# One PSUM bank for the last three scale/shift sums, and the steps around it, in a fused fp32 transformer kernel

## The chip, the core and the metric

The kernel runs on one core of a Trainium2 chip. The metric is the device time of one execution in microseconds (us), taken as the median of several. The profile adds one execution in which the hardware profiler recorded every instruction. TensorE is called PE in it, VectorE DVE, ScalarE ACT, GpSimd POOL, and SyncE, which issues the weight loads, SP.

## What is computed

A first block (adaptive-norm transformer block with two attention branches and an MLP) is followed by a second one of two layers (SwiGLU feed-forwards, a pooling mixer, latent attention). The sequence has 256 tokens, the width is 1024, and from the second block on 16 meta tokens stand ahead of the 256. The change touches the second half of the first block and its handover:

```python
mod = cs @ ada_w[l] + ada_b[l]
shift1, scale1, gate1, shift2, scale2, gate2 = jnp.split(mod, N_MOD, axis=-1)
...
merged = jax.nn.sigmoid(ga) * ya + jax.nn.sigmoid(gb) * yb
x = x + gate1[:, None, :] * (merged @ w_out[l])
h2 = modulate(rmsnorm(x, norm2_g[l]), shift2, scale2)
y = jnp.square(jax.nn.relu(h2 @ w_mlp_in[l])) @ w_mlp_out[l]
x = x + gate2[:, None, :] * y
...
h = jnp.concatenate([meta, x], axis=1)
h = h + 0.5 * swiglu(rmsnorm_2(h, ffn1_norm[l]), ffn1_w_gate[l], ffn1_w_up[l], ffn1_w_down[l])
```

Everything is fp32.

## The kernel before

**Precision and weights.** Each fp32 factor is split into a high part (fp32r) and the remainder, and a product is made of three matmuls (lines 564 to 566): high by high, remainder by high, high by remainder. The weights are one stream of chunks of 128x1024 values (512 KB), in the order of use. SP loads chunk c into slot c mod 8 of `raw`. ACT writes the high part of a chunk into `whi` (line 1010), DVE the remainder into `wlo` (line 1343); both have 5 slots. The chunks that are split carry their own numbers ("split 44" is chunk 84). The chunks of `ada_w` are not split: DVE multiplies them by the conditioning vector and sums (`ada_piece`, lines 1363 and 1366), two products a chunk. SP loads chunk c only when chunk c-8 has been consumed: for a split chunk by its `wlo`, for one of `ada_w` by its two products. SP's loads are one queue in order, so one that waits holds back all behind it.

**Groups.** A matrix product is cut into groups of two output tiles, each 128 outputs by 256 tokens: `wout0` to `wout3` (8 input tiles, 48 matmuls, two chunks each), `mlp_in0` to `mlp_in15` (48 matmuls, two chunks), `mlp_out0` to `mlp_out3` (32 input tiles, 192 matmuls, eight chunks). A group's sums lie in one of two PSUM pairs, G0 and G1. `pair_plan` lists all users of the pairs in order, they take them in turn, and `pair(name)` makes PE wait until the user two places earlier has been read by DVE (or ACT). Behind a group, DVE reads it: for `wout` and `mlp_out` this is `residual` (line 1397), then ACT makes `xh` (line 1031) and DVE `xl` (line 1404), the two parts of the next input; for `mlp_in` it is a scaling with `rstd` (line 1581).

**Scale/shift sums.** `mod7`, `mod10` and `mod11` are the last three of eight groups of columns of `mod` summed in this way (mod7 belongs to shift2, mod10 and mod11 to gate2). `mod_sum` on PE turns the 128x512 partial sums by four transposes (line 600) into PSUM; `mod_out` on DVE reduces them (line 1377) and adds the bias (line 1379). They are users of the pairs: mod7 stands behind wout1, mod10 behind mlp_in7, mod11 behind mlp_out0. So the group that follows each of them gets the pair of the group that ended just before it: wout2 that of wout1, mlp_in8 that of mlp_in7, mlp_out1 that of mlp_out0. Four more banks, A0 to A3, serve the attention, the means and the first gate/up group (`gu01`) of each SwiGLU, which uses A1 and A2.

**What sets the order.** Each engine's program is written out by hand; the engines meet by semaphores. `splits(name)` issues the splits up to a number that the plan gives for that group (`hi_to`, `lo_to`), so that ACT and DVE run ahead of PE. In wout0 DVE first makes the gain (`mod_gain`), then the ada piece (7, 3) (chunk 81), then the remainders of splits 44, 45 and 46 (the two chunks of wout1 and the first of wout2). ACT loads the table of Sqrt (`preload`) ahead of the high parts of splits 45 to 47. The meta tokens are scaled, split and squared on DVE and ACT in mlp_out0's turn, between `mod_out("mod11")` and the residual of mlp_out0, since all residuals of mlp_out wait for mod11. The groups after these are mlp_in0 behind wout3 (its first chunk is split 50) and mlp_in1 (its first chunk is split 52).

Of the kernel before, what the change touches and what calls it, by code (L numbers as in the profile page):

```python
# [251 lines left out]
MOD_ORDER = ["mod4", "mod5", "mod8", "mod9", "mod6", "mod7", "mod10", "mod11"]  # L252
HEAD_MODS = {4: "mod5", 8: "mod8", 12: "mod9", 16: "mod6"}
# [19 lines left out]
def pair_plan():  # L273
# [10 lines left out]
    out += [("wout0", 0, 2), ("wout1", 0, 2), ("mod7", 0, 1), ("wout2", 0, 2), ("wout3", 0, 2)]  # L284
    for i in range(FF1 // 2):
        out += [(f"mlp_in{i}", 0, 1)] + ([("mod10", 0, 1)] if i == 7 else [])
    out += [("mlp_out0", 0, 2), ("mod11", 0, 1)] + [(f"mlp_out{i}", 0, 2) for i in (1, 2, 3)]
# [21 lines left out]
class Plan:  # L309


    def __init__(self):
# [37 lines left out]
        order = [u[0] for u in users]  # L350
        for first, then in (("mod7", "wout1"), ("mod10", "mlp_in7"), ("mod11", "mlp_out0")):
            order.remove(first)
            order.insert(order.index(then), first)
        by = {u[0]: u for u in users}
        a = d = 0
        for name in order:
            a, d = a + by[name][1], d + by[name][2]
            self.left_act[name], self.left_dve[name] = a, d


def build_program(nc, xT, metaT, vecs, consts, bias_oh, bias_rows, wstream, scratch, outT):
# [6 lines left out]
    with ctx:  # L368
# [89 lines left out]
        out_done, mod_set = sem("out_done"), sem("mod_set")  # L458
# [81 lines left out]
        def tensor_program(e):  # L540
# [53 lines left out]
            def mod_sum(name, i, n=1):  # L594
                out = pair(name)
                for t in range(4 * n):
                    if t % 4 == 0:
                        e.wait_ge(ada_total, ADA_ORDER.index(i + t // 4) + 1)
                    acc = ada_sets[ADA_SET[i + t // 4]][0][:, t % 4 * P:(t % 4 + 1) * P]
                    m = e.transpose(out[:, 0, t * P:(t + 1) * P], acc, ident)  # L600
                m.then_inc(mod_summed, 1)
# [149 lines left out]
            for i in range(4):  # L751
                g = pair(f"mlp_out{i}")

                def ready(kt):
                    if i == 0 and kt % 2 == 0:
                        e.wait_ge(hid_lo, kt // 2 + 1)
                gemm(f"mlp_out{i}", [g[:, t, 0:SEQ] for t in range(2)], hid1, ready)
                if i == 0:
                    mod_sum("mod11", 11)
# [36 lines left out]
            e.wait_ge(pT1_done, HEADS1)  # L796
# [202 lines left out]
        def scalar_program(e):  # L999
# [123 lines left out]
            for i in range(4):  # L1123
                splits(f"brb{i}")
                if i:
                    merged_high(i - 1)
            merged_high(3)


            preload(ACT.Sqrt)  # L1130
            for i in range(4):
                splits(f"wout{i}")
                if i == 0:
                    e.wait_ge(gain_done, 2)
                if i == 1:
# [30 lines left out]
            for i in range(4):  # L1166
                splits(f"mlp_out{i}")
                if i == 0:
                    e.wait_ge(meta_scaled, 1)
                    e.activation(xh[:, :, 0:META], scaled_m, ACT.Copy).then_inc(meta_hi, 1)  # L1170
                    e.wait_ge(gain_done, 3)
# [162 lines left out]
        def vector_program(e):  # L1334
# [39 lines left out]
            def mod_out(name, n=1):  # L1374
                i = int(name[3:])
                e.wait_ge(mod_summed, MOD_ORDER.index(name) + 1)
                e.tensor_reduce(mod[:, 4 * i:4 * i + 4], G[plan.pair[name]][:, 0, :].rearrange("p (t d) -> p t d", t=4), AX_X, ALU.add).then_inc(left_dve, 1)
                e.wait_ge(left_dve, plan.left_dve[name])
# [151 lines left out]
            for i in range(4):  # L1530
# [19 lines left out]
            for i in range(4):  # L1550
                if i == 0:
                    ada_piece(*ADA_BRANCH[3])
                splits(f"wout{i}")
# [12 lines left out]
            for i in range(FF1 // 2):  # L1566
# [5 lines left out]
                if i == 7:  # L1572
                    mod_out("mod10")
# [8 lines left out]
                if i:  # L1582
                    hidden_low(i - 1)
            hidden_low(FF1 // 2 - 1)
# [4 lines left out]
            for i in range(4):  # L1589
                splits(f"mlp_out{i}")  # L1590
                if i == 0:
                    mod_out("mod11")
# [9 lines left out]
                    e.wait_ge(left_dve, plan.left_dve["mod11"])  # L1602
                residual("mlp_out", i, COLS1, lambda kt: mod[:, 5 * KT + kt:5 * KT + kt + 1])
                x_lo("ffn1_0", i, COLS1, lambda kt: g1m[:, kt:kt + 1])

# [447 lines left out]
```

## Time and profile before

| | us |
|---|---|
| median of 3 executions | 1317.89 |
| lowest, highest | 1317.29, 1320.47 |
| the profiled execution | 1315.07 |
| its span from first to last record | 1313.7 |

| engine | busy us | share of the span |
|---|---|---|
| PE | 1245.2 | 95% |
| DVE | 898.9 | 68% |
| ACT | 632.7 | 48% |
| POOL | 183.5 | 14% |

A row of the timeline gives start and duration in us, the engine, the line, the operation with its output and inputs, how many instructions it stands for, and in brackets how long the engine sat idle before it and what released it. Matmuls overlap in the array, so a matmul's duration is longer than its distance to the next; the distance from start to start is the time it costs. PEclk is the granted clock of PE, 1.00 being 2.4 GHz and 0.50 being 1.2 GHz.

### The profile page before, as it was taken

Reading aid. Unit: us, or ns where it says so; the run is one execution under the profiler, and the core shown is the slowest. Engines: PE = TensorE matmul, PEld = TensorE weight load, DVE = VectorE, ACT = ScalarE, POOL = GpSimd, SP = SyncE. Lnnn points to the kernel's source line nnn. Section 1 sums busy time; section 2 is a strip of 40 time slices with the busy share of each in tenths; the row PEclk is TensorE's granted clock in tenths of the full one; section 3 lists DMA queues with packets and bytes.
Section 4 is the critical chain, followed back from the end, with each engine's and each line's share of the span. In section 5 each row is a group of like instructions: output and inputs, shape, how many; then the busy total and the mean of one; then the engine's idle time right before and its main releaser. Section 6 shows DMA issues by size and latency. Waiting matters only on the chain.

```text
span 1313.7 us, 23695 instructions
## 1 busy us (share of the span) xinstructions
PE 1245.2 (95%) x9876; PEld 1210.4 (92%) x9876; DVE 898.9 (68%) x1283; ACT 632.7 (48%) x973; POOL 183.5 (14%) x181
## 2 busy tenths in 40 slices
PE   4999998999999999999799999989999999999996
PEld 3988898999899999999799999989999977999996
DVE  7969888777456766655966666676666664866653
ACT  4545544666344444443544444444445454644531
POOL 2014524000123000012300001210001220000022
PEclk7999999999999999999899999989999998999998
DMA  8956564666665555555245565445655531556540
GB/s 324 379 198 213 198 236 145 243 222 241 184 187 161 161 189 167 178 175 177 79 160 179 175 191 172 154 142 193 193 186 184 187 119 49 178 192 193 181 157 32
DMA packets 66994, 238.87 MB, mean 182 GB/s; under 512 B 7302, under 2 KB 9528, under 8 KB 66888
## 3 DMA queue, kind: packets, MB, share of 16 engines
q1 hardware_dynamic: 66296, 235.17, 53.7%
q0 software_dynamic: 592, 2.19, 0.5%
q8 instruction: 78, 1.28, 0.4%
q14 instruction: 28, 0.23, 0.0%
HBM read 236.26 MB, written 1.07 MB: 181 GB/s over the span
## 4 chain that ended last, share of the span: by engine, by line
PE 83%; DVE 11%; ACT 2%; issue 2%; DMA 1%; POOL 1%; SPq 0%; DVEq 0%; ACTq 0%
PE G L564 25%; PE G L565 25%; PE G L566 25%; DVE sb_wlo L1343 3%; DVE sb_hidf L1426 1%; DMA sb_raw<-in_wstream 1%; PE G L584 1%; DVE sb_rstd L1389 1%; PE A L691 1%; PE A L667 1%; ACT sb_whi L1010 1%; DMA sb_X<-in_xT 0%; DVE sb_xl L1846 0%; PE A L584 0%; ACT sb_p L1306 0%
## 5 line engine op out<-in xcount | busy, mean ns | idle before, releaser
L1343 DVE TENSOR_TENSOR sb_wlo<-sb_raw,sb_whi 128x1024 fp32r<-128x1024 f32 x395 | 488.5, 1269 | 94.0 <-ACT sb_whi L1010 93.7
L564 PE MATMUL G<-sb_xh,sb_whi 128*128 128x256 f32 (+2 forms) x1764 | 503.0, 285 | 13.7 <-DVE sb_gu L1634 7.5
L565 PE MATMUL G<-sb_xl,sb_whi 128*128 128x256 f32 (+2 forms) x1764 | 502.0, 285 | 0.0
L566 PE MATMUL G<-sb_xh,sb_wlo 128*128 128x256 f32 (+2 forms) x1764 | 500.6, 284 | 0.0
L1010 ACT ACTIVATE sb_whi<-sb_raw 128x1024 fp32r<-128x1024 f32 x395 | 404.6, 1050 | 197.9 <-PE G L566 169.2
L564 PEld LDWEIGHTS G<-sb_xh,sb_whi 128*128 128x128 f32 x1764 | 333.7, 189 | 17.6 <-DVE sb_gu L1634 8.4
L566 PEld LDWEIGHTS G<-sb_xh,sb_wlo 128*128 128x128 f32 x1764 | 333.6, 189 | 0.0
L565 PEld LDWEIGHTS G<-sb_xl,sb_whi 128*128 128x128 f32 x1764 | 333.3, 189 | 0.1
L564 PE MATMUL G<-sb_hh,sb_whi 128*128 128x256 f32 (+1 forms) x1056 | 300.2, 284 | 8.9 <-DVE sb_X L1397 6.3
L566 PE MATMUL G<-sb_hh,sb_wlo 128*128 128x256 f32 (+1 forms) x1056 | 299.4, 283 | 0.0
L565 PE MATMUL G<-sb_hl,sb_whi 128*128 128x256 f32 (+1 forms) x992 | 280.9, 283 | 0.0
L564 PEld LDWEIGHTS G<-sb_hh,sb_whi 128*128 128x128 f32 x1056 | 200.0, 189 | 9.9 <-DVE sb_X L1397 6.8
L566 PEld LDWEIGHTS G<-sb_hh,sb_wlo 128*128 128x128 f32 x1056 | 199.9, 189 | 0.0
L565 PEld LDWEIGHTS G<-sb_hl,sb_whi 128*128 128x128 f32 x992 | 187.3, 189 | 0.0
L1194 ACT ACTIVATE sb_gu<-sb_gu 128x272 f32<-128x272 f32 (+1 forms) x88 | 37.4, 425 | 196.5 <-DVE sb_gu L1634 194.0
L1634 DVE TENSOR_TENSOR sb_gu<-G,sb_rstd 128x544 f32<-128x544 f32 (+1 forms) x84 | 59.4, 707 | 63.3 <-PE G L566 63.3
L1874 POOL TENSOR_TENSOR sb_sumsq<-sb_X 128x256 f32<-128x256 f32 (+1 forms) x6 | 3.7, 620 | 700.4 <-DVE sb_X L1397 700.4
L1638 DVE TENSOR_TENSOR sb_hidf<-sb_gu 128x272 f32<-128x272 f32 (+1 forms) x88 | 38.2, 434 | 49.9 <-ACT sb_gu L1194 49.9
L1641 DVE TENSOR_TENSOR sb_hl<-sb_hidf,sb_hh 128x272 fp32r<-128x272 f32 (+1 forms) x88 | 38.2, 434 | 43.2 <-ACT sb_hh L1196 43.2
L1879 POOL TENSOR_TENSOR sb_sq<-sb_X 128x256 f32<-128x256 f32 (+1 forms) x42 | 33.0, 786 | 206.9 <-DVE sb_X L1397 206.9
L1196 ACT ACTIVATE sb_hh<-sb_hidf 128x272 fp32r<-128x272 f32 (+1 forms) x88 | 37.4, 424 | 49.6 <-DVE sb_hidf L1638 49.6
L1882 POOL TENSOR_TENSOR sb_sumsq<-sb_sumsq,sb_sq 128x256 f32<-128x256 f32 (+1 forms) x43 | 47.4, 1102 | 3.4
(299 smaller groups left out, 1276.8 us busy)
## 6 DMA issues: line engine op xcount, KB each, us to landing
sb_raw<-in_wstream SPq DMA_DIRECT2D x443, 512.0 KB, 4.4
sb_bias<-bias_scratch POOLq DMA_DIRECT2D x1, 2048.0 KB, 16.7
sb_X<-in_xT SPq DMA_DIRECT2D x2, 512.0 KB, 6.5
out_T<-sb_X SPq DMA_DIRECT2D x4, 256.0 KB, 2.2
sb_con<-in_consts SPq DMA_DIRECT2D x1, 632.0 KB, 7.3
sb_vec<-in_vecs SPq DMA_DIRECT2D x1, 82.5 KB, 1.9
sb_X<-in_metaT POOLq DMA_DIRECT2D x1, 64.0 KB, 4.7
sb_boh<-in_bias_oh SPq DMA_DIRECT2D x1, 51.0 KB
```

Source lines behind the costliest of these rows:

```text
L564: e.matmul(out, w_h, xs, start=k0 + s.kt == 0, stop=False)
L565: e.matmul(out, w_h, xr, start=False, stop=False)
L566: m = e.matmul(out, w_l, xs, start=False, stop=k0 + s.kt == ktotal - 1)
L1010: e.activation(whi[:, i % NSPLIT, 0:w], raw[:, c % NRAW, 0:w], ACT.Copy).then_inc(hi_done, 1)
L1194: e.activation(gu[:, b, 0, 0:n], gu[:, b, 0, 0:n], ACT.Silu).then_inc(silu_done, 1)
L1196: e.activation(hh[:, j * n:(j + 1) * n], hidf[:, b, 0:n], ACT.Copy).then_inc(hid_hi, 1)
L1343: e.tensor_tensor(wlo[:, i % NSPLIT, 0:w], raw[:, c % NRAW, 0:w], f(whi[:, i % NSPLIT, 0:w]), ALU.subtract).then_inc(lo_done, 1)
L1634: e.tensor_tensor(gu[:, b, :, 0:n], G[plan.pair[name]][:, :, 0:n], rb, ALU.mult).then_inc(left_dve, 1)
L1638: e.tensor_tensor(hidf[:, b, 0:n], gu[:, b, 0, 0:n], gu[:, b, 1, 0:n], ALU.mult).then_inc(hid_mul, 1)
L1641: e.tensor_tensor(hl[:, sl], hidf[:, b, 0:n], f(hh[:, sl]), ALU.subtract).then_inc(hid_lo, 1)
L1879: e.tensor_tensor(s, src, src, ALU.mult).then_inc(sumsq_done, 1)
L1882: e.tensor_tensor(sumsq[:, cols], sumsq[:, cols], s, ALU.add).then_inc(sumsq_done, 1)
```

## The change

It has four parts.

1. `mod7`, `mod10` and `mod11` leave the list of the pairs' users and get bank A2. PE waits for `pT1_done` (the attention's last read of that bank) ahead of mod7 and for `mod_read` (DVE's reduction of the one before) ahead of the others; the first SwiGLU waits for three of `mod_read`. Three users fewer means that each group from wout2 on waits for the group two places earlier, and that the groups between the three change pairs.
2. On DVE, mod10's reduction moves behind the scaling of mlp_in7 and the remainder of mlp_in6. On PE, mod11's transposes move from behind mlp_out0 to behind mlp_out1, and on DVE its reduction to behind `x_lo` of mlp_out1. The residuals of mlp_out0 and mlp_out1 wait for mod10's result alone, those of mlp_out2 and mlp_out3 for mod11's.
3. In wout0, DVE makes the three remainders ahead of the ada piece; ACT makes its three high parts ahead of the load of the Sqrt table, which goes to wout3. `split_hi` and `split_lo` up to wout0's last chunk are also called ahead of `merged_high(3)` and `merged_low(3)`.
4. The meta tokens' four steps on DVE and one on ACT move from mlp_out0's turn to mlp_out1's.

```diff
+OWN_BANK = ("mod7", "mod10", "mod11")
...
-    out += [("wout0", 0, 2), ("wout1", 0, 2), ("mod7", 0, 1), ("wout2", 0, 2), ("wout3", 0, 2)]
+    out += [("wout0", 0, 2), ("wout1", 0, 2), ("wout2", 0, 2), ("wout3", 0, 2)]
     for i in range(FF1 // 2):
-        out += [(f"mlp_in{i}", 0, 1)] + ([("mod10", 0, 1)] if i == 7 else [])
-    out += [("mlp_out0", 0, 2), ("mod11", 0, 1)] + [(f"mlp_out{i}", 0, 2) for i in (1, 2, 3)]
+        out.append((f"mlp_in{i}", 0, 1))
+    out += [(f"mlp_out{i}", 0, 2) for i in range(4)]
...
             def mod_sum(name, i, n=1):
-                out = pair(name)
+                if name in OWN_BANK:
+                    out = A[2][:, :].unsqueeze(1)
+                    if name == OWN_BANK[0]:
+                        e.wait_ge(pT1_done, HEADS1)
+                    else:
+                        e.wait_ge(mod_read, OWN_BANK.index(name))
+                else:
+                    out = pair(name)
...
-                if i == 0:
+                if i == 1:
                     mod_sum("mod11", 11)
...
-            e.wait_ge(pT1_done, HEADS1)
+            e.wait_ge(mod_read, len(OWN_BANK))
             swiglu("ffn1_0", final_factor)
...
+            split_hi(steps["wout0"][-1].i)
             merged_high(3)
...
-            preload(ACT.Sqrt)
             for i in range(4):
                 splits(f"wout{i}")
                 if i == 0:
                     e.wait_ge(gain_done, 2)
+                if i == 3:
+                    preload(ACT.Sqrt)
...
                 splits(f"mlp_out{i}")
                 if i == 0:
+                    e.wait_ge(gain_done, 3)
+                if i == 1:
                     e.wait_ge(meta_scaled, 1)
                     e.activation(xh[:, :, 0:META], scaled_m, ACT.Copy).then_inc(meta_hi, 1)
-                    e.wait_ge(gain_done, 3)
...
+            split_lo(steps["wout0"][-1].i)
             merged_low(3)
...
             for i in range(4):
+                splits(f"wout{i}")
                 if i == 0:
                     ada_piece(*ADA_BRANCH[3])
-                splits(f"wout{i}")
...
-                if i == 7:
-                    mod_out("mod10")
...
                 if i:
                     hidden_low(i - 1)
+                if i == 7:
+                    mod_out("mod10")
...
-                if i == 0:
-                    mod_out("mod11")
+                if i == 1:
                     mx, mg = X[:, :, 0:META], V("ffn1_norm0", 0, KT).unsqueeze(2).broadcast_to([P, KT, META])
...
-                    e.wait_ge(left_dve, plan.left_dve["mod11"])
+                if i == 0:
+                    e.wait_ge(mod_set, MOD_ORDER.index("mod10") + 1)
+                if i == 2:
+                    e.wait_ge(mod_set, MOD_ORDER.index("mod11") + 1)
                 residual("mlp_out", i, COLS1, lambda kt: mod[:, 5 * KT + kt:5 * KT + kt + 1])
                 x_lo("ffn1_0", i, COLS1, lambda kt: g1m[:, kt:kt + 1])
+                if i == 1:
+                    mod_out("mod11")
```

What moves on DVE at wout0, before. `sb_sc` and `sb_p` with `sb_raw` are the two products of the ada piece, `sb_wlo` the remainders of the weights; the row of `sb_X` is the residual of wout0.

```order
285 L1384 TENSOR_TENSOR sb_g1m<-sb_g1m,sb_vec 128x8 [waits gain_done]
286 L1366 SCALAR_TENSOR_TENSOR sb_sc<-sb_raw,sb_csil,sb_sc 128x512 [waits ada_acc,loaded1]
287 L1366 SCALAR_TENSOR_TENSOR sb_p<-sb_raw,sb_csil,sb_p 128x512 [waits ada_acc]
288 L1372 TENSOR_TENSOR sb_sc<-sb_sc,sb_p 128x512 [waits ada_acc]
289 L1343 TENSOR_TENSOR sb_wlo<-sb_raw,sb_whi 128x1024 [waits hi_done] x3
290 L1397 SCALAR_TENSOR_TENSOR sb_X<-G,sb_mod,sb_X 128x256 [waits mm_done]
```

The same stretch of DVE now:

```order
285 L1394 TENSOR_TENSOR sb_g1m<-sb_g1m,sb_vec 128x8 [waits gain_done]
286 L1349 TENSOR_TENSOR sb_wlo<-sb_raw,sb_whi 128x1024 [waits hi_done] x3
287 L1372 SCALAR_TENSOR_TENSOR sb_sc<-sb_raw,sb_csil,sb_sc 128x512 [waits ada_acc,loaded1]
288 L1372 SCALAR_TENSOR_TENSOR sb_p<-sb_raw,sb_csil,sb_p 128x512 [waits ada_acc]
289 L1378 TENSOR_TENSOR sb_sc<-sb_sc,sb_p 128x512 [waits ada_acc]
290 L1407 SCALAR_TENSOR_TENSOR sb_X<-G,sb_mod,sb_X 128x256 [waits mm_done]
```

The three remainders stand ahead of the ada piece; nothing is added, and no split stands ahead of `mod_gain` that was not there before.

What moves on DVE between mlp_out0 and mlp_out1, before (`sb_mod<-G` is mod11's reduction, the rows down to `sb_sumsq` the meta tokens):

```order
393 L1343 TENSOR_TENSOR sb_wlo<-sb_raw,sb_whi 128x1024 [waits hi_done] x8
394 L1377 TENSOR_REDUCE sb_mod<-G 128x4 [waits mod_summed]
395 L1379 TENSOR_TENSOR sb_mod<-sb_mod,sb_vec 128x4 [waits left_dve]
396 L1596 TENSOR_TENSOR sb_hidf<-sb_X,sb_vec 128x128 [waits hid_lo,meta_in]
397 L1598 TENSOR_TENSOR sb_xl<-sb_hidf,sb_xh 128x8x16 [waits meta_hi]
398 L1599 TENSOR_TENSOR sb_hidf<-sb_X 128x128
399 L1601 TENSOR_REDUCE sb_sumsq<-sb_hidf 128x16 [waits meta_sq]
400 L1397 SCALAR_TENSOR_TENSOR sb_X<-G,sb_mod,sb_X 128x256 [waits mm_done,left_dve]
```

The same stretch now, on to the end of mlp_out1's turn:

```order
393 L1349 TENSOR_TENSOR sb_wlo<-sb_raw,sb_whi 128x1024 [waits hi_done] x8
394 L1407 SCALAR_TENSOR_TENSOR sb_X<-G,sb_mod,sb_X 128x256 [waits mm_done,mod_set]
395 L1407 SCALAR_TENSOR_TENSOR sb_X<-G,sb_mod,sb_X 128x256
396 L1414 SCALAR_TENSOR_TENSOR sb_xl<-sb_X,sb_g1m,sb_xh 128x256 [waits xh_done] x2
397 L1349 TENSOR_TENSOR sb_wlo<-sb_raw,sb_whi 128x1024 [waits hi_done] x8
398 L1606 TENSOR_TENSOR sb_hidf<-sb_X,sb_vec 128x128 [waits hid_lo,meta_in]
399 L1608 TENSOR_TENSOR sb_xl<-sb_hidf,sb_xh 128x8x16 [waits meta_hi]
400 L1609 TENSOR_TENSOR sb_hidf<-sb_X 128x128
401 L1611 TENSOR_REDUCE sb_sumsq<-sb_hidf 128x16 [waits meta_sq]
402 L1407 SCALAR_TENSOR_TENSOR sb_X<-G,sb_mod,sb_X 128x256 [waits mm_done]
403 L1407 SCALAR_TENSOR_TENSOR sb_X<-G,sb_mod,sb_X 128x256
404 L1414 SCALAR_TENSOR_TENSOR sb_xl<-sb_X,sb_g1m,sb_xh 128x256 [waits xh_done] x2
```

The residual of mlp_out0 is now the first thing behind the eight remainders; the meta tokens and mod11 stand behind the next eight.

## Rows read from the trace of the kernel before

**Rows 1.** The page: busy us of each engine, share of span, instructions

```profile
PE 1245.2 (95%) x9876; PEld 1210.4 (92%) x9876; DVE 898.9 (68%) x1283; ACT 632.7 (48%) x973; POOL 183.5 (14%) x181
```

**Rows 2.** PE's timeline, last matmul of wout0, first of wout1

```profile
201.41 0.28 PE L566 MATMUL G<-sb_hh,sb_wlo 128*128 128x256 f32 x1
...
203.58 0.35 PE L564 MATMUL G<-sb_hh,sb_whi 128*128 128x256 f32 x1 [1.89 <-DVE sb_wlo L1343]
```

**Rows 3.** PE's timeline, mod7's transposes and the start of wout2

```profile
209.27 0.60 PE L600 MATMUL G<-sb_con,sb_sc 128*128 128x128 f32 x4
212.90 0.39 PE L564 MATMUL G<-sb_hh,sb_whi 128*128 128x256 f32 x1 [3.03 <-DVE sb_X L1397]
...
216.64 0.31 PE L564 MATMUL G<-sb_hh,sb_whi 128*128 128x256 f32 x1
```

**Rows 4.** PE's timeline, mod10's transposes and the start of mlp_in8

```profile
272.10 0.60 PE L600 MATMUL G<-sb_con,sb_gu 128*128 128x128 f32 x4
274.35 0.38 PE L564 MATMUL G<-sb_xh,sb_whi 128*128 128x258 f32 x1 [1.66 <-DVE sb_hidf L1581]
```

**Rows 5.** PE's timeline, mod11's transposes and the start of mlp_out1

```profile
342.73 0.60 PE L600 MATMUL G<-sb_con,sb_gu 128*128 128x128 f32 x4
346.58 0.58 PE L564 MATMUL G<-sb_hh,sb_whi 128*128 128x256 f32 x1 [3.24 <-DVE sb_X L1397]
...
349.73 0.32 PE L566 MATMUL G<-sb_hh,sb_wlo 128*128 128x256 f32 x1
```

**Rows 6.** Busy time by stretch: PE, PEld, DVE, ACT, POOL, then PEclk, DMA share, GB/s

```profile
212.90:216.60 3.70, 3.70 (x18) 3.70 (x19) 2.92 (x3) 1.44 (x3) 3.48 (x4) 0.55 0.39 134
...
346.50:349.80 3.30, 3.22 (x15) 3.23 (x16) 2.74 (x5) 2.38 (x5) 3.22 (x4) 0.50 0.01 2
```

**Rows 7.** DVE's timeline, from the ada piece in wout0 to mlp_in0

```profile
200.17 0.74 DVE L1366 SCALAR_TENSOR_TENSOR sb_sc<-sb_raw,sb_csil,sb_sc 128x512 f32<-128x512 f32 x1
...
202.22 3.49 DVE L1343 TENSOR_TENSOR sb_wlo<-sb_raw,sb_whi 128x1024 fp32r<-128x1024 f32 x3
...
211.97 0.87 DVE L1397 SCALAR_TENSOR_TENSOR sb_X<-G,sb_mod,sb_X 128x256 f32<-128x256 f32 x2
...
214.32 1.63 DVE L1343 TENSOR_TENSOR sb_wlo<-sb_raw,sb_whi 128x1024 fp32r<-128x1024 f32 x1
220.37 0.88 DVE L1397 SCALAR_TENSOR_TENSOR sb_X<-G,sb_mod,sb_X 128x256 f32<-128x256 f32 x2 [4.42 <-PE G L566]
...
222.72 3.31 DVE L1343 TENSOR_TENSOR sb_wlo<-sb_raw,sb_whi 128x1024 fp32r<-128x1024 f32 x2
...
229.95 2.35 DVE L1343 TENSOR_TENSOR sb_wlo<-sb_raw,sb_whi 128x1024 fp32r<-128x1024 f32 x2
```

**Rows 8.** PE's timeline, the first matmul of mlp_in1

```profile
231.76 0.47 PE L564 MATMUL G<-sb_xh,sb_whi 128*128 128x258 f32 x1
```

**Rows 9.** ACT's timeline in wout0 and wout1

```profile
199.26 1.28 ACT L1020 ACT_TABLE_LOAD   x1
...
207.02 1.99 ACT L1010 ACTIVATE sb_whi<-sb_raw 128x1024 fp32r<-128x1024 f32 x2
...
211.63 0.22 ACT L1138 ACTIVATE sb_xh<-sb_mod 128x16 fp32r<-128x16 f32 x1 [2.62 <-DVE sb_mod L1379]
```

**Rows 10.** SP's load at 201.60 alone, then the one at 205.7: us from issue to landing

```profile
DMA to landing us min/median/max: 3.6/3.6/3.6
...
DMA to landing us min/median/max: 6.4/6.4/6.4
```

**Rows 11.** DVE's timeline, the reading of mlp_in8

```profile
280.40 0.16 DVE L1579 COPY sb_shift_out<-G 128x2 f32<-128x2 f32 x1 [2.44 <-PE G L566]
```

**Rows 12.** DVE's timeline: meta tokens, residuals of mlp_out1 and mlp_out2

```profile
344.18 0.29 DVE L1596 TENSOR_TENSOR sb_hidf<-sb_X,sb_vec 128x128 f32<-128x128 f32 x1
...
370.74 0.88 DVE L1397 SCALAR_TENSOR_TENSOR sb_X<-G,sb_mod,sb_X 128x256 f32<-128x256 f32 x2 [3.22 <-PE G L566]
...
393.14 0.88 DVE L1397 SCALAR_TENSOR_TENSOR sb_X<-G,sb_mod,sb_X 128x256 f32<-128x256 f32 x2 [3.22 <-PE G L566]
```

More of the change, by code:

```diff
@@ L348, in __init__ @@
             self.pair[f"gate{i}"] = self.pair[f"gate{i - 1}"]
[L350 to L354, printed above, removed]
         a = d = 0
-        for name in order:
-            a, d = a + by[name][1], d + by[name][2]
+        for name, for_act, for_dve in users:
+            a, d = a + for_act, d + for_dve
             self.left_act[name], self.left_dve[name] = a, d
@@ L457, in build_program @@
         v_act, v_dve, rows_set, wo_tile = sem("v_act"), sem("v_dve"), sem("rows_set"), sem("wo_tile")
-        out_done, mod_set = sem("out_done"), sem("mod_set")
+        out_done, mod_set, mod_read = sem("out_done"), sem("mod_set"), sem("mod_read")
         SUMSQ = {n: 15 * (k + 1) for k, n in enumerate(("wout", "mlp_out", "ffn1_0", "ffn2_0"))}
@@ L1376, in mod_out @@
                 e.wait_ge(mod_summed, MOD_ORDER.index(name) + 1)
-                e.tensor_reduce(mod[:, 4 * i:4 * i + 4], G[plan.pair[name]][:, 0, :].rearrange("p (t d) -> p t d", t=4), AX_X, ALU.add).then_inc(left_dve, 1)
-                e.wait_ge(left_dve, plan.left_dve[name])
+                if name in OWN_BANK:
+                    e.tensor_reduce(mod[:, 4 * i:4 * i + 4], A[2][:, :].rearrange("p (t d) -> p t d", t=4), AX_X, ALU.add).then_inc(mod_read, 1)
+                    e.wait_ge(mod_read, OWN_BANK.index(name) + 1)
+                else:
+                    e.tensor_reduce(mod[:, 4 * i:4 * i + 4], G[plan.pair[name]][:, 0, :].rearrange("p (t d) -> p t d", t=4), AX_X, ALU.add).then_inc(left_dve, 1)
+                    e.wait_ge(left_dve, plan.left_dve[name])
                 e.tensor_tensor(mod[:, 4 * i:4 * i + 4], mod[:, 4 * i:4 * i + 4], V("ada_b", 4 * i, 4), ALU.add).then_inc(mod_set, 1)
```

## The prediction, made before the changed kernel ran

> **What bounds the kernel now.** I read the page first. PE is busy for 95% of the span, DVE for 68% [rows 1], so time can only be won where PE stands still or runs slow. Then PE's timeline between wout0 and the first SwiGLU, looking for brackets. Between matmuls that follow each other without a pause the distance from start to start is 0.117 us: mlp_out2 is 192 matmuls and takes 393.14 - 370.74 = 22.40 us [rows 12]. Against this step four places stand out:
>
> - wout1 starts 2.17 us after the last matmul of wout0 and waited for a remainder of weights [rows 2]. Loss 2.17 - 0.12 = 2.05.
> - wout2 waits 3.03 us behind mod7's transposes, for the residual of wout1, whose pair it takes [rows 3]. Then 18 steps take 216.64 - 212.90 = 3.74 us where 18 x 0.117 = 2.10 would do: another 1.64. The granted clock there is 0.55, most of the stretch at 1.2 GHz [rows 6].
> - mlp_in8 waits 1.66 us for the reading of mlp_in7 [rows 4]; no slow stretch follows.
> - mlp_out1 waits 3.24 us for the residual of mlp_out0, behind which stand mod11 and the meta tokens [rows 5, 12]. Then 14 steps take 3.15 us instead of 1.63, another 1.52, at a granted clock of 0.50 [rows 6].
>
> So the clock fell after the waits of 3.03 and 3.24 us and not after those of 1.66 and 1.89. If all of it went, 2.05 + 3.03 + 1.64 + 1.66 + 3.24 + 1.52 = 13.1 us would be won.
>
> **wout0 to mlp_in1.** Two edits act here. First, DVE makes the remainders before the ada piece: the first of the three (3.49 / 3 = 1.16 each) then starts at 200.17 instead of 202.22 [rows 7], ends at 201.33, and PE, which is done with wout0 at 201.53, no longer waits. ACT's high parts come 1.4 us sooner too, by the table load that moves away [rows 9]. The two new calls of split_hi and split_lo issue nothing: the splits up to wout0's last chunk stand ahead of that place already, and the order of the instructions shows none moved there. Second, wout2 now takes the pair of wout0, whose residual is long done, and wout3 that of wout1.
>
> PE without waits would then run wout1 from 201.53 to 207.13 (48 x 0.117 = 5.60), mod7 to 207.73 (0.60), wout2 to 213.33, wout3 to 218.93. The residual of wout1 ends at 211.97 + 0.87 = 212.84 [rows 7], and DVE is no sooner and no later than before, since the same work in another order stands ahead of it; so wout3 is free 0.5 us before PE wants it. Its second chunk is wanted at 213.33 + 2.80 = 216.13, and its remainder ends at 214.32 + 1.63 = 215.95 [rows 7]; PE starts some 0.2 us after a remainder ends (203.38 to 203.58 [rows 2, 7]), so this is just in time.
>
> From there DVE is what is late. Before, it paused 4.42 us ahead of the residual of wout2 [rows 7]; from 200.17 to the first remainder of mlp_in1 that is its only pause that PE's pace makes, and all work in between stays. That remainder is the first of the two at 229.95 and ends at 231.13 [rows 7]. Without the pause it ends at 226.71, and mlp_in1 can start at 226.91 instead of 231.76 [rows 8]: **gain 4.85 us**. The rest of 6.72 (2.05 + 3.03 + 1.64) remains as two new waits: 1.2 us ahead of mlp_in0, whose first remainder (half of the 3.31 us at 222.72 [rows 7]) comes at 224.38 - 4.42 + 0.2 = 220.16 against 218.93, and 0.6 us ahead of mlp_in1. It follows that the sooner remainders are worth next to nothing by themselves: they only move PE's wait from wout1 to mlp_in0.
>
> What the swap costs. The ada piece ends 3.5 us later (its two products at 205.10 instead of 201.60), and SP's load of chunk 89, which needs that slot, stands behind it, with five more loads behind that one in SP's queue. Issued at 205.10, chunk 89 lands 3.6 us later [rows 10], at 208.7. ACT wants it at 208.0, as the second of the two high parts at 207.02 [rows 9], and is then done at 209.8; its next work, mod7's shift, comes at 211.63 after a wait of 2.62 [rows 9]. So nothing is lost, priced at nothing under this wait; with the 6.4 us of the last load in that burst [rows 10] it would be 0.9 us late. I take 3.6, since chunk 89 is at the head of the queue and the DMA engines are idle then. The table load of 1.28 us [rows 9] now stands in wout3 ahead of the xh of wout3; ACT waited 2.6 us and more for residuals all along, so nothing again.
>
> **mlp_in8.** It takes the pair of mlp_in6, free long before, and starts right behind the transposes: **gain 1.7 us** (the 1.66 and 0.1 of a slow first step). DVE does the reduction of mod10 (some 0.9 us) later; it had 2.44 us to spare one group on [rows 11], so no new wait.
>
> **mlp_out1.** It takes the pair of mlp_in15 and starts right behind mlp_out0: **gain 3.24 + 1.52 = 4.8 us**. Three chunks are split ahead, 8.4 us of work for PE, and the residual and xl of mlp_out0 take DVE 2.3 us. The transposes of mod11 (0.60) come behind mlp_out1 and cost the same there. The meta tokens take DVE from 344.18 to the residual, about 1.5 us [rows 12]; they now fall into the 3.22 us in which DVE waits for the end of mlp_out1 [rows 12]. If ACT held them up, only that residual would be late, and mlp_out3 wants its pair 22 us later.
>
> **Downstream** all groups change pairs, but keep their distances; I price this at nothing. The sum is 4.85 + 1.7 + 4.8 = **11.4 us**. Against the profiled execution, 1315.07, this gives 1303.7; that execution lies 2.8 under the median of 1317.89, and as medians are compared the forecast is 1317.9 - 11.4 = **1306.5 us**.
>
> **Bounds and rivals.** For the first term: 4.85 hangs on remainders that take 1.6 us beside POOL's work and 1.16 alone [rows 7]; with all four in that stretch at 1.16 it rises by at most the 1.9 that is left, and a later chunk 89 takes 0.9 off. So 9.5 to 13.1 for the sum.
>
> - *The new waits bring the clock down.* The two (1.2 and 0.6 us) come within 8 us; each fall costs some 1.6, as in [rows 3, 5, 6]. Then 1308.1 or 1309.7. Against it: 1.66 and 1.89 did not do it. The Trainium skill, page "TensorE: Matmul & The Clock Gate", section "A second HAM failure mode: psum-queue depth-cycling", tells of a kernel in which micro-idles between groups of matmuls were enough to make the clock swing; by that rule this rival is what happens, and the falls here came after the long waits alone.
> - *All waits go.* Remainders run faster without POOL beside them: 1317.9 - 13.1 = 1304.8.
> - *The change doesn't do what it says.* PE's stops at wout2 and mlp_out1 are not for the pair but for something that comes just as late, and only the 1.7 of mlp_in8 comes: 1316.2. Against it: the rows name the residual, and its end (212.84) and PE's start (212.90) lie 0.06 apart [rows 3, 7].
> - *Slower.* Chunk 89 and the five loads behind it land late. The place is ACT's second high part in wout1: from a landing of 5.5 us after issue each us is lost one for one down the DVE chain to mlp_in1, plus 1.6 once PE's wait is long enough for the clock to fall. The sign turns at 5.5 + 11.4 - 1.6 = 15.3 us; at 20 us the kernel takes 1322.6. Against it: 6.4 is the longest in that burst [rows 10].
>
> **Chances.** Forecast (9.5 to 13 us won) 0.80; clock falls 0.08; all waits go 0.06; doesn't do what it says 0.04; slower 0.02. The first three are faster by over 0.3% (4.0 us, about what a measurement of this kernel can tell from no change): 0.94. Within 0.3%: 0.04. Slower: 0.02. The range takes in the full gain and one to two falls of the clock, and a median that may lie an us to either side (the three before span 3.2 us): 1303.2 to 1310.
>
> **What would show it.** In the profile after: no bracket at wout1, wout2, mlp_in8 and mlp_out1, and PEclk 1.00 there; brackets of about 1.2 and 0.6 us ahead of mlp_in0 and mlp_in1, released by line 1349, the remainders; DVE without a pause from 200 us to there; mlp_in1 starting 4.9 us sooner than 231.76; SP's load burst at 205.1. Wrong I would be if wout3 waited for the residual of wout1 (then 0.5 us of slack was too little), if the clock fell at mlp_in0, or if a stop showed up behind mlp_out3, where the meta tokens and mod11 are wanted.

## The result

The changed kernel takes 1305.71 us in the median of 4 executions (1303.46 to 1307.76), the kernel before 1318.09 us (1317.29 to 1320.47). The medians lie 12.4 us apart. The ratio of the executions is 0.9902 with a 95% interval of 0.9885 to 0.9919, that is 12.9 us (10.7 to 15.2) less. Forecast were 1306.5 us and 11.4 us less.

The page of the profile after (busy us, share of the span, instructions), against [rows 1]:

```profile
span 1306.4 us, 23696 instructions
...
PE 1248.9 (96%) x9876; PEld 1211.8 (93%) x9876; DVE 898.9 (69%) x1283; ACT 632.9 (48%) x973; POOL 182.7 (14%) x181
```

This execution is the slowest of the four, 1307.76 us, and its span is only 7.3 us shorter than before. Where the change acts, more was won (12.01 us, below). The difference between the two has another cause, which the repeated profiles of the unaltered kernels show (end of the experiments). PE's timeline after, from wout0 to the first means of the SwiGLU. The columns are start, duration, engine, line, operation, and in brackets the idle time before and its releaser; line 560 is line 564 of before, 603 is 600, 1349 is 1343:

```profile
200.92 0.39 PE L560 MATMUL G<-sb_hh,sb_whi 128*128 128x256 f32 x1 [0.26 <-DVE sb_hh L1539]
...
202.43 0.36 PE L560 MATMUL G<-sb_hh,sb_whi 128*128 128x256 f32 x1
...
208.12 0.60 PE L603 MATMUL A<-sb_con,sb_sc 128*128 128x128 f32 x4
208.47 0.36 PE L560 MATMUL G<-sb_hh,sb_whi 128*128 128x256 f32 x1
...
220.84 0.36 PE L560 MATMUL G<-sb_xh,sb_whi 128*128 128x258 f32 x1 [0.85 <-issue]
...
227.67 0.36 PE L560 MATMUL G<-sb_xh,sb_whi 128*128 128x258 f32 x1 [0.41 <-DVE sb_wlo L1349]
...
267.90 0.60 PE L603 MATMUL A<-sb_con,sb_gu 128*128 128x128 f32 x4
268.25 0.36 PE L560 MATMUL G<-sb_xh,sb_whi 128*128 128x258 f32 x1
...
359.01 0.60 PE L603 MATMUL A<-sb_con,sb_gu 128*128 128x128 f32 x4
359.36 0.36 PE L560 MATMUL G<-sb_hh,sb_whi 128*128 128x256 f32 x1
...
411.62 0.70 PE L588 MATMUL A<-sb_sumsq,sb_mean_ones 128*128 128x272 f32 x2 [0.76 <-issue]
```

The brackets of [rows 2, 3, 4, 5] at these places are gone. wout1 (202.43), wout2 (208.47) and mlp_in8 (268.25) start without a pause, and mlp_out1 has no row of its own any more: mod11's transposes stand one group later (359.01), behind it. Two small brackets are new, 0.85 us ahead of mlp_in0 (220.84) and 0.41 us ahead of mlp_in1 (227.67). The granted clock (the third number from the end) is 1.00 in both stretches, where [rows 6] had 0.55 and 0.50:

```profile
199.00:220.00 21.00, 20.71 (x172) 20.31 (x172) 19.29 (x29) 11.32 (x16) 8.52 (x11) 1.00 0.58 222
...
336.00:412.00 76.00, 75.24 (x640) 74.83 (x638) 47.18 (x53) 33.86 (x43) 24.74 (x23) 1.00 0.55 175
```

DVE after, in the stretch of [rows 7]:

```profile
201.06 3.49 DVE L1349 TENSOR_TENSOR sb_wlo<-sb_raw,sb_whi 128x1024 fp32r<-128x1024 f32 x3
204.47 0.74 DVE L1372 SCALAR_TENSOR_TENSOR sb_sc<-sb_raw,sb_csil,sb_sc 128x512 f32<-128x512 f32 x1
...
212.87 0.87 DVE L1407 SCALAR_TENSOR_TENSOR sb_X<-G,sb_mod,sb_X 128x256 f32<-128x256 f32 x2
...
215.21 1.63 DVE L1349 TENSOR_TENSOR sb_wlo<-sb_raw,sb_whi 128x1024 fp32r<-128x1024 f32 x1
216.76 0.87 DVE L1407 SCALAR_TENSOR_TENSOR sb_X<-G,sb_mod,sb_X 128x256 f32<-128x256 f32 x2
...
219.11 3.30 DVE L1349 TENSOR_TENSOR sb_wlo<-sb_raw,sb_whi 128x1024 fp32r<-128x1024 f32 x2
...
226.31 2.35 DVE L1349 TENSOR_TENSOR sb_wlo<-sb_raw,sb_whi 128x1024 fp32r<-128x1024 f32 x2
```

The pause of 4.42 us ahead of the residual of wout2 is gone (216.76 follows the remainder of 215.21 at once), and the durations are those of before. PE starts mlp_in0 at 220.84 and mlp_in1 at 227.67 right behind the first remainders of the pairs at 219.11 (the first of the two took 1.63 us) and 226.31. The trace names the remainder as releaser at mlp_in1 alone (at mlp_in0 it says `issue`); that mlp_in0 waits for its remainder too is shown by the experiment that moves it, DVE reordered further.

All stretches are told from one mark, since the executions reach wout0 at times up to 1.3 us apart: the second bracket in wout0 (0.26 us, behind the last merged remainder), 200.02 in the profile of before and 200.92 after. From it to the second mean of the SwiGLU (422.73 before, [0.77 <-issue]; 411.62 after) it was 222.71 us and is 210.70: **12.01 us less**. The expectations call that last row the first mean (the mean of line 588 with 256 columns just before it is not counted there).

### The profile page after: what moved, and what is told of

It reads as the page before. It is cut to its first block, busy times and chain, and to the rows that moved or that the text cites. A ratio compares the mean times of both kernels' runs of the same rounds, so it can differ in the third digit from the quotient of the medians.

```text
span 1306.4 us, 23696 instructions
## 1 busy us (share of the span) xinstructions
PE 1248.9 (96%) x9876; PEld 1211.8 (93%) x9876; DVE 898.9 (69%) x1283; ACT 632.9 (48%) x973; POOL 182.7 (14%) x181
## 4 chain that ended last, share of the span: by engine, by line
PE 82%; DVE 12%; ACT 2%; issue 2%; DMA 2%; POOL 1%; SPq 0%; DVEq 0%; ACTq 0%
PE G L560 25%; PE G L561 25%; PE G L562 24%; DVE sb_wlo L1349 3%; DMA sb_raw<-in_wstream 2%; DVE sb_hidf L1436 1%; PE G L580 1%; DVE sb_rstd L1399 1%; PE A L694 1%; PE A L670 1%; ACT sb_whi L1013 0%; DVE sb_xl L1861 0%; PE A L580 0%; DVE sb_X L1724 0%; PE A L681 0%
## 5 line engine op out<-in xcount | busy, mean ns | idle before, releaser
L1407 DVE SCALAR_TENSOR_TENSOR sb_X<-G,sb_X 128x272 f32<-128x272 f32 (+1 forms) x32 | 12.4, 428 | 51.5 <-PE G L562 51.5
```

## The experiments

All results are told by the same mark. The table has the distance in us from it to the first matmul of mlp_in0, the first of mlp_in1 and the second mean of the SwiGLU, each the difference of two starts in PE's timeline, and whether PE's clock was at 0.5 right behind wout1's start.

| kernel | mlp_in0 | mlp_in1 | second mean | clock fell at wout1 |
|---|---|---|---|---|
| before | 25.75 | 31.74 | 222.71 | no |
| before, second profile | 26.49 | 32.48 | 225.37 | yes |
| after | 19.92 | 26.75 | 210.70 | (no wait) |
| after, second and third profile | 19.92, 19.92 | 26.75, 26.74 | 210.69, 210.69 | (no wait) |
| part 3 undone | 22.44 | 28.42 | 212.49 | yes |
| part 3 alone | 26.70 | 32.68 | 223.75 | (no wait) |
| meta tokens later alone | 26.48 | 32.47 | 222.06 | yes |
| mod7's bank alone | 20.93 | 26.92 | 217.93 | no |
| mod11's bank alone | 26.94 | 32.93 | 218.93 | no |
| bank alone, all three | 22.45 | 28.44 | 212.51 | yes |
| DVE reordered further | 18.89 | 26.33 | 210.28 | (no wait) |
| after, two more DVE products | 21.80 | 28.62 | 212.57 | (no wait) |
| before, two more DVE products | 26.51 | 32.51 | 223.57 | yes |

### mod7's bank alone

```diff
+OWN_BANK = ("mod7",)
-    out += [("wout0", 0, 2), ("wout1", 0, 2), ("mod7", 0, 1), ("wout2", 0, 2), ("wout3", 0, 2)]
+    out += [("wout0", 0, 2), ("wout1", 0, 2), ("wout2", 0, 2), ("wout3", 0, 2)]
```

> The kernel before with mod7 alone in the bank of its own (mod10 and mod11 stay users of the pairs, nothing else moves). Theory (the pair is what wout2 waits for, and DVE's work limits what is won): no wait at wout2, no slow clock there, a wait at wout1 of 1.9 us as before, mlp_in1 starts 4.8 us sooner; time 1318.1 - 4.8 = 1313.3; the waits at mlp_in8 (1.66) and mlp_out1 (3.24, then 1.5 of slow clock) as before. Rival (wout2's stop is not for the pair): 1318.1.

Measured: 1314.45 us in the median (ratio 0.9972, 0.9952 to 0.9992). mlp_in1 comes at 26.92 instead of 31.74 us: 4.82 us sooner, where 4.8 was expected. The profile has no bracket at wout2, and the later ones are those of before:

```profile
204.26 0.36 PE L565 MATMUL G<-sb_hh,sb_whi 128*128 128x256 f32 x1 [1.89 <-DVE sb_wlo L1351]
...
270.21 0.39 PE L565 MATMUL G<-sb_xh,sb_whi 128*128 128x258 f32 x1 [1.65 <-DVE sb_hidf L1593]
...
342.44 0.58 PE L565 MATMUL G<-sb_hh,sb_whi 128*128 128x256 f32 x1 [3.24 <-DVE sb_X L1409]
```

The pair is what wout2 waited for. With the wait at wout1 still there mlp_in0 starts 1.01 us later than with the whole change (20.93 against 19.92) and without a bracket, but mlp_in1 only 0.17 us later: what the sooner remainders win at wout1 is given back at mlp_in0 and mlp_in1, as the prediction had it.

### Part 3 undone, and part 3 alone

```diff
             for i in range(4):
-                splits(f"wout{i}")
                 if i == 0:
                     ada_piece(*ADA_BRANCH[3])
+                splits(f"wout{i}")
```

The load of the Sqrt table goes back ahead of wout0's high parts with it; the second kernel is the kernel before with the reverse of both.

> The changed kernel with part 3 undone: in wout0 DVE makes the ada piece ahead of the three remainders again, and ACT loads the Sqrt table ahead of its high parts. Theory (DVE's chain of work sets the start of mlp_in1, the sooner remainders only move PE's wait): PE waits 1.9 us at wout1 again, the waits at mlp_in0 and mlp_in1 shrink from 0.85 and 0.41 us to nothing or nearly so, mlp_in1 starts within 0.2 us of where it does with part 3; time within 0.3 us of the changed kernel, 1305.7. Rival (the sooner remainders are a gain of their own): mlp_in1 starts 2.05 us later, time 1307.8.

> The kernel before with part 3 alone. Theory: wout1 starts 2.05 us sooner, and PE gives it back at wout2, where the wait for the residual of wout1 grows from 3.03 to about 5.1 us, since DVE reaches that residual no sooner; a slow stretch of the clock behind it as before (1.6 us); time 1318.1, as before. Rival (worth 2.05 us by itself): 1316.0.

Measured: part 3 undone 1308.62 us (0.9936, 0.9915 to 0.9958), part 3 alone 1317.5 us (1.0004, 0.9989 to 1.0019). Alone it wins nothing: PE gives all back at wout2, with a wait of 5.07 us where 5.1 was expected.

```profile
213.53 0.58 PE L564 MATMUL G<-sb_hh,sb_whi 128*128 128x256 f32 x1 [5.07 <-DVE sb_X L1398]
```

Undone in the changed kernel it costs 1.67 us at mlp_in1 (28.42 against 26.75), not the 0.2 that the theory allowed. The reason is the clock, not DVE. The wait of 1.89 us at wout1 was followed by a stretch at half speed in this execution, and was not in that with mod7's bank alone; first the row of part 3 undone, then that of mod7's bank alone (granted clock 0.61 and 1.00):

```profile
203.10:207.50 4.40, 4.30 (x23) 4.33 (x24) 4.15 (x6) 1.80 (x4) 1.55 (x3) 0.61 0.98 380
```

```profile
204.20:208.50 4.30, 4.24 (x36) 4.27 (x37) 4.06 (x6) 1.70 (x4) 1.49 (x3) 1.00 0.97 361
```

In 4.4 us PE did 23 matmuls, where it did 36 in 4.3 us. 15 steps took 0.214 instead of 0.117 us, 1.5 us in all. Without the fall part 3 is worth the 0.17 us of the row above, with it 1.67 (1.79 by the second mean). The high times of this kernel have a further cause: its profiled execution, the slowest of five at 1312.52 us, stood at half speed in the second attention for longer than any other (47.7 us for a stretch of 40.9, see the end of the experiments). Both theory and rival had their number wrong: the sooner remainders win hardly anything by themselves, but they take away a wait behind which the clock falls in some executions.

### The bank alone for all three sums, and mod11's bank alone

> The kernel before with the bank of its own for all three sums, and no step moved otherwise (part 1 alone). Theory: the stretch from wout0 to the first mean of the SwiGLU, 224.6 us before and 212.6 with the whole change, takes 212.6 to 212.9 where no fall of the clock adds 1.5 us, 214.2 where one does behind the wait of 1.9 us at wout1; parts 2 to 4 are worth under 0.3 us. DVE's reduction of mod10 stands ahead of the reading of mlp_in7 and costs nothing, since mlp_in9 alone needs that pair. Rival (each part carries its share): 215 us or more without a fall.

> The kernel before with mod11 alone in the bank of its own; its transposes stay behind mlp_out0, and DVE still does mod11 and the meta tokens ahead of the residual of mlp_out0 (parts 2 and 4 left out there). Theory (only the pair stops mlp_out1, and nobody waits for that residual any more): no wait and no slow clock at mlp_out1, 4.8 us less from wout0 to the first mean of the SwiGLU, as much as the whole change wins there; time 1318 - 4.8 = 1313. Rival (the move of mod11 and of the meta tokens is needed): some 1.5 us less of it.

The first differs from the second by its list:

```diff
-OWN_BANK = ("mod11",)
+OWN_BANK = ("mod7", "mod10", "mod11")
```

Measured: all three 1306.72 us (0.9924, 0.9902 to 0.9946), mod11 alone 1311.4 us (0.9955, 0.9935 to 0.9975). With all three, the stretch takes 212.51 us with a fall of the clock at wout1. The expectation counted from the bracket ahead of the mark, 1.9 us sooner (hence its 224.6 and 212.6 us for 222.71 and 210.70); counted so it is 412.82 - 198.41 = 214.41 us, where 214.2 was expected with a fall. It agrees to 0.02 us with part 3 undone. So parts 2 and 4 are worth nothing measurable, and part 3 the 0.17 or 1.67 us above. mod10's bank was not tried alone. Its share can be read from mlp_in1 to mlp_in8: 42.59 us before and with mod7's bank alone, 40.70 with all three.

With mod11's bank alone, the way from mlp_in8 (276.45) to the second mean (419.86) is 143.41 us; before it was 422.73 - 274.35 = 148.38, and after 411.62 - 268.25 = 143.37. The whole 4.97 us comes from the pair, though DVE still does mod11 and the meta tokens ahead of the residual. This execution lost 1.2 us of it at wout2, where the slow stretch lasted 27 steps instead of 18 (mlp_in1 at 32.93 instead of 31.74).

### The meta tokens later, alone

```diff
                 if i == 0:
                     mod_out("mod11")
+                    e.wait_ge(left_dve, plan.left_dve["mod11"])
+                if i == 1:
                     mx, mg = X[:, :, 0:META], V("ffn1_norm0", 0, KT).unsqueeze(2).broadcast_to([P, KT, META])
```

> The kernel before with part 4 alone: the meta tokens move to mlp_out1's turn, mod11 keeps its place in the pairs. Theory: DVE reaches the residual of mlp_out0 1.5 us sooner, so PE waits 1.75 instead of 3.24 us at mlp_out1; if the clock falls only behind waits of 3 us, the slow stretch of 1.5 us goes too: gain 3.0 us, 1315.1. Rival for the clock (it falls behind shorter waits as well): gain 1.5 us, PEclk near 0.5 behind the wait of 1.75.

Measured: 1315.26 us (0.9991, 0.9975 to 1.0006), not told apart from before. The wait at mlp_out1 is 1.78 us as expected, but the clock fell behind it all the same, 1.4 us later (PEclk 1.00, then 0.50):

```profile
345.90:347.30 1.40, 1.36 (x11) 1.36 (x12) 0.85 (x2) 1.40 (x5) 1.32 (x3) 1.00 0.00 0
347.30:350.60 3.30, 3.30 (x18) 3.30 (x17) 3.13 (x3) 1.12 (x2) 3.15 (x3) 0.50 0.14 37
```

From mlp_in8 (275.18) to mlp_out1 (345.94) it is 70.76 us instead of 72.23: 1.47 us won, and none by the clock. The rival for the clock was right here.

### Two more products on DVE

```diff
             for i in range(4):
+                if i == 2:
+                    for _ in range(2):
+                        e.tensor_tensor(sig[:, 0:2, :], sig[:, 0:2, :], sig[:, 0:2, :], ALU.mult).then_inc(padded, 1)
```

> The changed kernel with two products of 128x512 added on DVE behind wout1's xl (their result is used by nobody). In all, two instructions of 0.6 us and a semaphore each, 1.3 us of DVE. Theory (from wout1 on DVE's chain is what PE waits for): one for one, the waits at mlp_in0 and mlp_in1 grow together by about 1.3 us and the stretch from wout0 to the first mean of the SwiGLU takes 212.0 instead of 210.7 us, if the clock does not fall. Rival (DVE has room there): 210.7.

> The kernel before with the same two products on DVE in the same place. Theory: they vanish in the 4.42 us in which DVE waits there for wout2; the stretch takes 222.7 us as before, or 1.5 more or less by one fall of the clock. Rival: 224.0.

One execution of each. In the changed kernel the products ran beside POOL's and took 2.24 us instead of 1.3:

```profile
214.40 2.24 DVE L1565 TENSOR_TENSOR sb_sig<-sb_sig 128x512 f32<-128x512 f32 x2
216.68 1.22 DVE L1350 TENSOR_TENSOR sb_wlo<-sb_raw,sb_whi 128x1024 fp32r<-128x1024 f32 x1
217.82 0.87 DVE L1408 SCALAR_TENSOR_TENSOR sb_X<-G,sb_mod,sb_X 128x256 f32<-128x256 f32 x2
```

The remainder behind them took 1.22 instead of 1.63 us, as it now ran without POOL. The residual of wout2 starts 17.72 us behind the mark instead of 15.85 (the third profile of the changed kernel), 1.87 us later, and the stretch takes 212.57 instead of 210.69, 1.88 us longer: one for one, though by more than expected, since the products were mis-sized. It does not come where it was expected. The waits at mlp_in0 and mlp_in1 stay as they were (0.87 and 0.40 us), and a new one stands inside wout3, ahead of its second chunk, whose remainder is the one behind the products:

```profile
217.95 0.39 PE L560 MATMUL G<-sb_hh,sb_whi 128*128 128x256 f32 x1 [1.65 <-DVE sb_wlo L1350]
```

The prediction had called that remainder just in time. The clock did not fall behind this wait (1.00). In the kernel before, the same products vanish: mlp_in1 stands 32.51 us behind the mark, and 32.48 in the second profile of the kernel before, which also has the fall at wout1. They went into DVE's pause ahead of the residual of wout2, 4.42 us in [rows 7]:

```profile
215.83 2.24 DVE L1554 TENSOR_TENSOR sb_sig<-sb_sig 128x512 f32<-128x512 f32 x2
218.10 1.22 DVE L1344 TENSOR_TENSOR sb_wlo<-sb_raw,sb_whi 128x1024 fp32r<-128x1024 f32 x1
221.89 0.88 DVE L1398 SCALAR_TENSOR_TENSOR sb_X<-G,sb_mod,sb_X 128x256 f32<-128x256 f32 x2 [2.57 <-PE G L566]
```

So DVE's chain is what PE waits for after the change and not before it.

### DVE reordered further

```diff
+                if i == 2:
+                    split_lo(steps["mlp_in0"][0].i)
                 residual("wout", i, COLS1, lambda kt: mod[:, 2 * KT + kt:2 * KT + kt + 1])
...
-                if i % 2 == 0:
+                if i % 2 == 0 and i:
                     ada_piece(*ADA_MLP[i // 2])
                 splits(f"mlp_in{i}")
+                if i == 0:
+                    ada_piece(*ADA_MLP[0])
```

> The changed kernel with two more steps moved on DVE: the remainder of mlp_in0's first chunk goes ahead of the residual of wout2, and the ada piece (10, 0) behind the two remainders of mlp_in1. Nothing is left out. Theory (DVE's chain is what PE waits for at mlp_in0 and mlp_in1): the wait of 0.85 us at mlp_in0 goes, the one of 0.41 us at mlp_in1 shrinks to at most 0.3, mlp_in1 starts 1.2 us sooner, time 1.2 us less than the changed kernel. Rival (the waits are for something else, say the residual of wout2, which now comes 1.2 us later): no gain, a wait released by line 1407 or by xl.

Measured: 1305.87 us (0.9918, 0.9900 to 0.9936), beside the changed kernel's 1304.47 on the same chip: no difference that shows. The stretch is 0.41 us shorter, a third of what was expected. The wait at mlp_in0 is gone (18.89 us against 19.92), but PE now stops inside mlp_in0, for an input part of wout3, and again at mlp_in1:

```profile
224.20 0.39 PE L560 MATMUL G<-sb_xh,sb_whi 128*128 128x258 f32 x1 [0.44 <-DVE sb_xl L1414]
...
226.72 0.36 PE L560 MATMUL G<-sb_xh,sb_whi 128*128 128x258 f32 x1 [0.36 <-DVE sb_wlo L1349]
```

ACT's timeline of this kernel shows why that part is late:

```profile
221.25 1.28 ACT L1023 ACT_TABLE_LOAD   x1
222.54 0.20 ACT L1023 ACTIVATE sb_warm<-sb_eps_c 128x1 f32<-128x1 f32 x1
222.65 0.90 ACT L1034 ACTIVATE sb_xh<-sb_X,sb_g1m 128x256 fp32r<-128x256 f32 x2
```

The residual of wout3 starts at 221.81, so its first half is there by 222.3, and ACT is still loading the Sqrt table that part 3 had put there. In the changed kernel ACT was done with that load 1.25 us before the residual of wout3 released its input part. One wait gone let the next come forward, first DVE's, then ACT's.

### The unaltered kernels again

> The changed kernel itself, unaltered, for a second profile and more times. Theory (the clock falls behind waits of some 2 us in some executions and not in others, by where the wait falls): the waits are the same to 0.1 us, while stretches at PEclk 0.5 stand in other places than in the first profile, and each moves the time by about 1.5 us; median 1305 to 1307. Rival (the clock answers to the length of a wait alone): the same slow stretches as in the first profile, behind the wait of 1.88 us at 650 among them.

> The kernel before, unaltered, for a second profile. Theory (whether the clock falls behind a wait of 1.9 us changes from execution to execution): the waits are the same, the slow stretches stand in part elsewhere than in the first profile. Rival (a program's falls are its own, fixed by the distances between its waits): slow stretches at wout2 and mlp_out1, none at wout1 and none behind the wait of 1.88 us in the second SwiGLU, 190.2 us from there to the next wait but one.

> The changed kernel, unaltered, for a third profile. Theory (as for the kernel before): a fall behind the 1.88 us wait in the second SwiGLU in some executions only, so perhaps none here. Rival (fixed by the program): the fall is there a third time, 191.7 us to the next wait but one. In the attention of the second block both expect 40.95 us or more, since the two profiles so far differ there (43.4 and 40.95).

Measured: the changed kernel 1304.47 us in the median of 6 (0.9908, 0.9893 to 0.9923), its third profile an execution of 1302.13 us, the second one of the kernel before an execution of 1319.77. The three profiles of the changed kernel agree to 0.01 us on the stretch (210.70, 210.69, 210.69), and their executions took 1307.76, 1304.64 and 1302.13 us. Most of what parts them stands behind the change, in two places, and both are the clock:

- In the second SwiGLU PE waits 1.88 us, in every profile. From there to the bracket of 0.27 us behind its last group it is 191.7 us in the first two profiles and 190.2 in the third. The stretch behind the wait, first profile (0.59), then that of the kernel with DVE reordered, which also took 190.2 (1.00):

```profile
649.90:654.10 4.20, 4.14 (x21) 4.15 (x22) 2.14 (x5) 1.94 (x5) 0.00 (x0) 0.59 0.08 31
```

```profile
648.90:653.10 4.20, 4.12 (x33) 4.13 (x34) 2.14 (x6) 1.92 (x5) 0.00 (x0) 1.00 0.08 34
```

- In the second attention, from the bracket of 0.47 to that of 0.30 us, it is 43.4 us in the first profile and 40.9 in the two others. The first profile shows 16 us at half speed there, of which these are two rows, and the second profile 1.00 at the same place:

```profile
1071.00:1075.00 4.00, 4.00 (x12) 1.97 (x10) 1.06 (x5) 2.31 (x7) 0.00 (x0) 0.50 0.10 41
...
1083.00:1087.00 4.00, 4.00 (x13) 2.76 (x13) 0.91 (x1) 2.04 (x6) 0.00 (x0) 0.50 0.00 0
```

```profile
1070.30:1074.30 4.00, 4.00 (x22) 2.41 (x21) 2.09 (x6) 3.21 (x8) 0.00 (x0) 1.00 0.10 41
```

The two places make 4.0 of the 5.6 us between the first and the third. Another 1.0 us lies ahead of the mark, and 0.7 us between the two places, behind a wait of 4.4 us, where the clock is back sooner in the third. They also close the account of the result: 12.01 us won in the stretch, less 0.90 for the later mark, 1.52 for the second SwiGLU (191.72 against 190.20 in the profile of before) and 2.41 for the attention (43.40 against 40.99), leaves 7.2 of the 7.3 us between the two spans.

The slow stretch in the second SwiGLU was there in the second profile too, as the rival had it; the attention, and in the third profile the SwiGLU, decide. So the theory holds and the rival falls: the same program with the same waits has its slow stretches now here and now there. The second profile of the kernel before says the same. It fell at wout1 (205.08 to 208.28), which the first had not, and then waited 2.23 instead of 3.03 us at wout2, since DVE had gone on in the meantime; mlp_out1 began slow as before. Its attention took 43.5 us, against 41.0 in the first. It has one thing more, which stays open: mlp_out2 took 395.50 - 372.46 = 23.04 us instead of the 22.40 of [rows 12], and mlp_out3 418.54 - 395.50 = 23.04 as well, a step of 0.120 us at a granted clock of 1.00. This is most of why its mlp_in8 to second mean took 150.30 us and not 148.38.

## Why the prediction was right

**The places and their causes** were right one by one. Distances in us, before to after, from mark to mark:

| stretch | before | after | won | forecast |
|---|---|---|---|---|
| mark to mlp_in1 | 31.74 | 26.75 | 4.99 | 4.85 |
| mlp_in1 to mlp_in8 | 42.59 | 40.58 | 2.01 | 1.7 |
| mlp_in8 to the second mean | 148.38 | 143.37 | 5.01 | 4.8 |

The forecast named 11.4 us and 12.0 were won. In the second and third stretch one term was mis-sized: the four transposes were booked at 0.60 us, their busy time in [rows 4, 5], while without a wait behind them the next matmul starts 0.35 us after the first of them (267.90 to 268.25, 359.01 to 359.36). That is 0.25 us each. In the first stretch the transposes decide nothing, since DVE sets the start of mlp_in1 there; its chain ended 0.12 us sooner than forecast (226.31 - 0.90 = 225.41 against 229.95 - 4.42 = 225.53).

**DVE's chain as the limit of the first term** was right and is shown from both sides: DVE's pause is gone and the remainders end where they were forecast (PE starts mlp_in0 19.92 us behind the mark; forecast were 220.16 - 200.02 = 20.14), and 1.87 us more work on DVE costs 1.88 us after the change and nothing before it. Of the two new waits the first, counted against PE's pace as the forecast did, is 220.84 - 219.71 - 0.12 = 1.01 us instead of 1.2 (219.71 is the start of wout3's last matmul); the second's bracket is 0.41 instead of 0.6. The brackets were to be released by the remainders of line 1349; the second is, the first says `issue`.

**The price of the swap** was right. SP's loads come later, chunk 89 lands when forecast, and ACT waits for it without anyone waiting for ACT. ACT's timeline after; the mark stands 0.9 us later here than before, so the forecast of 208.7 is 209.6:

```profile
209.69 1.06 ACT L1013 ACTIVATE sb_whi<-sb_raw 128x1024 fp32r<-128x1024 f32 x1 [0.73 <-DMA sb_raw<-in_wstream]
212.52 0.22 ACT L1143 ACTIVATE sb_xh<-sb_mod 128x16 fp32r<-128x16 f32 x1 [1.77 <-DVE sb_mod L1389]
```

ACT still idled 1.77 us ahead of mod7's shift, where it had 2.62 [rows 9].

**The meta tokens** were priced too low, under a wait that hid it. DVE takes 2.8 us for them in mlp_out1's turn (355.90 to 358.67), not 1.5, since it waits 1.57 us there for ACT's high part; before, it was 0.37. Of the 3.22 us of pause ahead of the residual of mlp_out1 0.55 are left, so PE did not notice.

**What was wrong** is the reading of the clock. "The clock fell after the waits of 3.03 and 3.24 us and not after those of 1.66 and 1.89" was true of one execution and is no rule. Behind the wait of 1.9 us at wout1 it fell in five of the eight profiles that have this wait; behind the 1.8 us at mlp_out1 with the meta tokens later it fell too. The wait of 1.66 us at mlp_in8 was followed by no slow stretch in any of the seven profiles that have it. Hence part 3 was priced at next to nothing and is worth 0.17 us in executions in which the clock stays up at wout1, and 1.67 in the others. For the sum it made no difference, since the profile of before was one without the fall there.

**The rivals.** That the new waits bring the clock down did not come true (1.00 up to the second mean in all three profiles of the changed kernel); the rule of the Trainium skill that the prediction cites (page "TensorE: Matmul & The Clock Gate", section "A second HAM failure mode: psum-queue depth-cycling"), told there of a bf16 kernel with matmuls of 512 columns, did not show here in waits of 0.85 and 0.41 us. That all waits go, that the pair was not the cause, and that chunk 89 comes late are each refuted by rows above.

**The median.** The forecast took 11.4 us off the median, and 12.0 were won in the stretch. The measured 12.9 us (10.7 to 15.2 by the interval) agree with both and cannot tell them apart. That the median of four came within 0.8 us of the forecast is in part luck: single executions of the changed kernel lie up to 5.6 us apart (1302.13 to 1307.76), mostly by slow stretches elsewhere.

## What to carry to other kernels

A small side job that borrows one of two alternating buffers makes the next large job wait for the buffer that was just filled; it is worth a buffer of its own even where the job is tiny. When a wait goes, ask which engine paused during it, for the work behind that pause is the next limit: here 6.7 us of waits and slow clock gave 5.0. And a single profile does not tell behind which waits the clock falls; price a wait of 2 us once without and once with a fall.

## What the runs showed of the hardware

- Behind one and the same wait of about 1.9 us, in the same program, PE's granted clock stays at 1.00 or goes to 0.5 for some 3.3 us (15 or 16 steps of 0.214 instead of 0.117 us), which costs 1.5 us. In the second SwiGLU, behind a wait of 1.88 us, this parts the fourteen profiles in two groups, six at 190.2 and eight at 191.7 us for the same stretch, with nothing between.
- From wout0 to the second mean, over all fourteen profiles, a slow stretch came behind each wait of 2.2 us (three of them), 3.0 (two), 3.2 (five) and 5.1 (one), and behind none of the eight of 1.65 us.
- The fall need not follow the wait at once: it came 1.4 us behind a wait of 1.78 us.
- A fall can cost less than its 1.5 us: before the change the one at wout1 cost 0.74 us at mlp_in1 (32.48 against 31.74), as DVE caught up meanwhile and the next wait was shorter.
- In the second attention, where PE's work is thin, one execution stayed at half speed for 16 us, which made the stretch 2.4 us longer. Three of the fourteen profiles have such a stretch (43.4, 43.5 and 47.7 us; the others 40.9 to 41.0).
- Two products of 128x512, the second waiting for the first, took DVE 2.24 us together, for most of it beside POOL's work; by half of the 1.16 us that a 128x1024 remainder takes alone [rows 7] it would be some 1.2 (an estimate, no run measured them alone).
